# Two mixer layers: exchange of halves issued by SyncE, two pairs of index banks, low-rank products in four row groups, and steps in other places

## What is computed

```
x = x + 0.5 * swiglu(rms_norm(x), ...)
p = rms_norm(x) @ w_in                    # 12 column tiles for attention, 15 for the two recurrences
ya = dsa_attention(pa)                    # index scores pick 128 keys per query, then softmax over them
yb = rwkv7_time_mix(pb); yc = gated_deltanet(pc)
x = x + concat(ya, yb, yc) @ w_out
x = x + 0.5 * swiglu(rms_norm(x), ...)
```

## Time and profile before

| | |
|---|---|
| median of 3 runs | 3539.54 us (3538.71 to 3545.95) |
| profiled execution | 3536.79 us, its span 3535.0 us |
| PE busy | 3386.3 us, 96% of the span |
| mean granted clock of PE | 0.98 |
| first block's projection stretches, layer 0 and layer 1 | 382 to 565.5 us, 1556 to 1740.5 us |

### The profile page before, as it was taken

One profiled execution on the slowest core, in us unless ns is written; L12 is line 12 of the kernel. 1 busy time (PEld: TensorE's weight loads), 2 busy tenths in 40 slices (PEclk: granted clock), 3 DMA queues, 4 the chain that ended last, 5 costly groups with the idle time before them and its releaser, 6 DMA issues.

```text
span 3535.0 us, 47369 instructions
## 1 busy us (share of the span) xinstructions
PE 3386.3 (96%) x16944; PEld 2781.0 (79%) x16944; DVE 1423.5 (40%) x2753; ACT 1255.4 (36%) x1890; POOL 1659.6 (47%) x2052
## 2 busy tenths in 40 slices
PE   7999998799999999999878999999899999999999
PEld 6888776688888888887658788878767888888887
DVE  5431588845221422137886532214563110341100
ACT  4222436434222422234553432223533332433321
POOL 6765542005665566554400366654404555535554
PEclk9999999899999999999989999999999999999999
DMA  5443321003443344333200244432202223213222
GB/s 183 143 147 107 104 87 55 13 7 120 147 145 117 122 146 143 119 104 93 66 25 1 72 148 146 134 108 78 72 1 78 95 95 99 73 66 101 95 98 99
DMA packets 104223, 340.49 MB, mean 96 GB/s; under 512 B 12144, under 2 KB 17936, under 8 KB 103968
## 3 DMA queue, kind: packets, MB, share of 16 engines
q1 hardware_dynamic: 83984, 277.83, 24.0%
q10 hardware_dynamic: 20112, 60.89, 5.4%
HBM read 330.78 MB, written 2.65 MB: 94 GB/s over the span
## 4 chain that ended last, share of the span: by engine, by line
issue 39%; POOL 32%; PE 27%; DVE 1%; POOLq 0%; ACT 0%; DMA 0%; SPq 0%; DVEq 0%
POOL w_lo L667 32%; PE ps L2212 7%; PE ps L2214 7%; PE ps L2213 7%; PE ps L2976 1%; PE ps L2955 1%; PE ps L2235 0%; PE ps L2964 0%; PE ps L2236 0%; PE ps L2240 0%; PE ps L3066 0%; DVE stat L2113 0%; DVE sq L2106 0%; PE ps L3072 0%; PE ps L2956 0%
## 5 line engine op out<-in xcount | busy, mean ns | idle before, releaser
L667 POOL TENSOR_TENSOR w_lo<-w_raw,w_hi 128x256 fp32r<-128x256 f32 x2040 | 1653.0, 842 | 1858.2 <-ACT w_hi L710 1852.5
L2212 PE MATMUL ps<-h_hi,w_hi 128*128 128x512 f32 x2608 | 1021.8, 392 | 1.4 <-ACT mem L938 1.4
L2214 PE MATMUL ps<-h_hi,w_lo 128*128 128x512 f32 x2608 | 1016.9, 390 | 0.0
L2213 PE MATMUL ps<-h_lo,w_hi 128*128 128x512 f32 x2608 | 1016.3, 390 | 0.0
L710 ACT ACTIVATE w_hi<-w_raw 128x1024 fp32r<-128x1024 f32 x510 | 538.3, 1057 | 903.1 <-DMA w_raw<-in_tiles 902.7
L2212 PEld LDWEIGHTS ps<-h_hi,w_hi 128*128 128x128 f32 x2608 | 490.7, 188 | 116.3 <-issue 6.8
L2214 PEld LDWEIGHTS ps<-h_hi,w_lo 128*128 128x128 f32 x2608 | 490.3, 188 | 103.4
L2213 PEld LDWEIGHTS ps<-h_lo,w_hi 128*128 128x128 f32 x2608 | 490.8, 188 | 100.9
L2213 PE MATMUL ps<-a_lo,w_hi 128*128 (+1 forms) x1120 | 437.0, 390 | 0.0
L2212 PE MATMUL ps<-a_hi,w_hi 128*128 (+1 forms) x1056 | 410.8, 389 | 0.0
L2214 PE MATMUL ps<-a_hi,w_lo 128*128 (+1 forms) x1056 | 410.8, 389 | 0.0
(11 more groups left out here) (470 smaller groups left out, 3617.1 us busy)
## 6 DMA issues: line engine op xcount, KB each, us to landing
w_raw<-in_tiles SPq DMA_DIRECT2D x510, 512.0 KB, 3.4
ada_raw<-in_ada_tiles ACTq DMA_DIRECT2D x96, 512.0 KB, 3.4
mem<-mem ACTq DMA_DIRECT2D x80, 64.0 KB, 2.0
x<-in_x_t SPq DMA_DIRECT2D x2, 1024.0 KB, 6.6
sq<-in_cond ACTq DMA_DIRECT2D x4, 512.0 KB, 4.0
mem<-gates SPq DMA_DIRECT2D x8, 256.0 KB, 4.1
consts<-in_consts SPq DMA_DIRECT2D x1, 1280.0 KB, 13.0
core_mem<-gates SPq DMA_DIRECT2D x8, 128.0 KB, 2.8
```

What stands on the lines that cost most here:

```text
L667: ins = nc.gpsimd.tensor_tensor(w_lo[:, s, part], w_raw[:, s, part], w_hi[:, s, part].bitcast(F32), ALU.subtract)
L2212: nc.tensor.matmul(bank, wh, hi, start=first, stop=False, skip_group_check=True)
L2213: nc.tensor.matmul(bank, wh, lo, start=False, stop=False, skip_group_check=True)
L2214: return nc.tensor.matmul(bank, wl, hi, start=False, stop=last, skip_group_check=True)
```

## The change

1. **Exchange of halves.** `swap_halves` moves from ACT's program into SP's. SP issues the four DMAs of a unit behind the load of a tile, once the unit's copy is done; all weight loads behind it in SP's queue follow.
2. **Index pairs.** Odd pairs use banks 2 and 3 and the ReLU buffers `U_Z`; even pairs keep 5, 6 and 43, 44. Waits on ReLUs and sums reach back four instead of two. Pairs 0 and 1 stand behind tile 6, pairs 2 and 3 behind tile 7, pair p behind tile p + 4 from there: the last is behind recurrent tile 3 and not 5.
3. **Low-rank.** The 64 rows of the third product are split into two groups of 32: eight matmuls in four row groups, with one wait between the first four and the last four, since the halves of one sum go to the same bank.
4. **Other places.** Key sums stand inside tile 13 and not behind it; their roots stand before the copy of tile 13, with the Sqrt table loaded earlier; the decays and their wait stand before the last copy; the rounding of the last tile's successor and the copy of `v_first` move into the attention loop. On DVE the rotations of keys and queries go from pairs 1 to 5 to pairs 3 to 7, `head_inverse` from pair 9 to pair 10, and eight selection rounds go ahead of the head scaling.

```diff
+        INDEX_TILES = {6: (0, 1), 7: (2, 3), **{p + 4: (p,) for p in range(4, len(INDEX_PAIRS))}}
+        def index_bank(p):
+            return 2 if p % 2 else 5
+        def relu_unit(p):
+            return U_Z if p % 2 else 43
...
+            def swap_halves(l, m):                                   # SP
+                unit = att_unit(m)
+                r = TURNS.index(unit)
+                if r >= 4:
+                    sp.wait_ge(S["roped"], 10 * l + r - 3)
+                sp.wait_ge(S["proj_out"], (ATT_TILES + REC_TILES) * l + m + 1)
+                turned = mem[:, U_TURNED[unit], :]
+                for at in range(0, P, HD):
+                    for to, of in ((at, at + HD // 2), (at + HD // 2, at)):
+                        sp.dma_start(turned[to:to + HD // 2, :], mem[of:of + HD // 2, unit, :]).then_inc(S[f"rot_moved{r % 4}"], 16)
...
+                load_tiles(start, att + RING)
+                for m in range(ATT_TILES):
+                    load_tile(att + m + RING)
+                    if m == 1:
+                        swap_halves(l, 0)
+                    if m and att_unit(m) in U_TURNED:
+                        swap_halves(l, m)
...
-                        if i >= 2:                                   # ACT, index_relus
-                            act.wait_ge(S["score_added"], i - 1)
-                        nc.scalar.activation(mem[:, 43 + x, 0:w], ps[:, 5 + x, 0:w], ACT.Relu)
+                        if i >= 4:
+                            act.wait_ge(S["score_added"], i - 3)
+                        nc.scalar.activation(mem[:, relu_unit(p) + x, 0:w], ps[:, index_bank(p) + x, 0:w], ACT.Relu)
-                    if att_unit(m) in U_TURNED:
-                        act.wait_ge(S["proj_out"], done)
-                        swap_halves(att_unit(m))
...
+                    if m == LORA_TILE + 1:                           # ACT, before the copy of tile m
+                        head_roots(7, 2, 1.0, EPS_L2)
+                    if m == LORA_TILE + 1:                           # ACT, behind the copy
+                        act.wait_ge(S["decay_in"], l + 1)
+                    if m < REC_TILES - 1:
+                        round_tile(base + m + 4)
+                    if i == 1:                                       # ACT, attention loop
+                        round_tile(BASE[f"rec_in{l}"] + REC_TILES - 1 + 4)
...
-                    if 1 <= p <= 5:                                  # DVE
+                    if 3 <= p <= 7:
-                        rope(U_K + p - 1).then_inc(S["roped"], 1)
+                        rope(U_K + p - 3).then_inc(S["roped"], 1)
-                    if p == 9:
+                    if p == 10:
                         head_inverse(mem[:, 33:38, :], 5)
+                best_keys(2, range(12, 16))
+                best_keys(1, range(4))
                 scale_heads((0, 1))
...
-                        for bank, rows in ((2, slice(0, 32)), (4, slice(32, 64)), (6, slice(64, 128))):
-                            ins = nc.tensor.matmul(ps[:, bank + c, :], lora[rows, l, blk(c)], lg[rows, :], start=True, stop=True)
+                        for row, bank, part in ((0, 2 + c, c), (32, 4 + c, c), (64, 6 + c, c), (96, 7 - c, 1 - c)):
+                            rows = slice(row, row + 32)
+                            ins = nc.tensor.matmul(ps[:, bank, :], lora[rows, l, blk(part)], lg[rows, :],
+                                                   start=row < 64 or c == 0, stop=row < 64 or c == 1, skip_group_check=True)
+                            if c == 0 and row >= 64:
+                                ins.then_inc(S["lora_ready"], 1)
+                                if row == 96:
+                                    pe.wait_ge(S["lora_ready"], 3 * l + 2)
```

More of the change, by code:

```diff
@@ L914, in index_relus @@
                         act.wait_ge(S["index_ready"], i + 1)
[L915 to L928 removed]
+                        if i >= 4:
+                            act.wait_ge(S["score_added"], i - 3)
+                        nc.scalar.activation(mem[:, relu_unit(p) + x, 0:w], ps[:, index_bank(p) + x, 0:w], ACT.Relu).then_inc(S["relu_ready"], 1)
                 for m in range(ATT_TILES):
@@ L2397, in index_scores @@
                         pe.wait_ge(S["roped"], roped0 + 2 + p)
-                    done = due("index", 2) - 2
-                    if done:
+                    done = due("index", 2) - 4
+                    if done > 0:
                         pe.wait_ge(S["relu_ready"], done)
@@ L2417, in attention @@
                         head_sum(m - 8)
-                    if index_pair(m) is not None:
-                        index_scores(index_pair(m))
+                    for p in index_pairs(m):
+                        index_scores(p)
                 due("proj_out", ATT_TILES)
@@ L2444, in attention @@
                         due("roped", 5)
-                    if index_pair(ATT_TILES + m) is not None:
-                        index_scores(index_pair(ATT_TILES + m))
+                    for p in index_pairs(ATT_TILES + m):
+                        index_scores(p)
                     if m == 0:
```

70 lines of the change are left out of this document (27 added, 43 removed).

## The result

| | before | after |
|---|---|---|
| median, runs beside each other | 3541.54 us (3538.71 to 3545.95, 4 runs) | 3514.73 us (3507.53 to 3516.75, 4 runs) |
| ratio, 95% interval | | 0.9923 (0.9908 to 0.9938) |
| profiled execution | 3536.79 us, span 3535.0 | 3516.75 us, span 3514.9 |
| mean granted clock of PE | 0.980 | 0.981 |

One of the ten executions of the run before_again, further down, had a granted clock of 0.55 and took 5705 us; it is left out there.

The account below looks back on a forecast made before the run. PE was taken as the bound, busy 3386 of 3535 us; gains of 8.6 (layer 0) and 9.2 us (layer 1), together 17.8, took 3536.8 to 3519.0, or 3521.7 for the median; own range 3515 to 3528, with rivals 3512 to 3532.

Parts of the forecast that it names:

- copies behind the exchange: Index part: PE's waits for ACT's copies behind the first exchange shrink, gaining 0.4 and 0.3 us in layers 0 and 1.
- ReLU waits at the index pairs: Index scores: PE's waits for ACT's ReLUs go whole with two pairs of banks, 2.6 and 3.2 us.
- half clock behind them and fewer places: Index part: half-clock stretches go with the ReLU waits, 1.7 us a layer; moving pairs itself put at nothing.
- wait at the spread: Spread of head norms: PE's wait for the last ReLU goes, 1.1 us a layer.
- low-rank products: Low-rank group: two slots of four products instead of four slots, 1.8 us gained a layer.
- start of the softmax: Softmax start: last copy comes sooner, most waits turn into one for the next exponentials; 1.0 and 1.1 us gained.
- first rival: Softmax start gives all it has: 6.4 us more from waits, some 3 from the clock, 3512 us; chance 0.12.
- The last sign: Softmax start: PE would then wait 2 us or more for an exponential.
- Exchange on SP: SP issues the halves instead of ACT: 2.4 us an exchange, landing up to 5.4 us, cost nothing.
- Moving pairs changes no count: Index pairs: still 24 small matmuls a layer, so moving them gains or costs nothing in itself.
- VectorE at the spreads: Spreads: DVE's inversion ends at 503.2, PE comes at 506.6, margin 3.4 us; rival that DVE becomes the bound, chance 0.12.
- Selection rounds: Head scaling: eight rounds ahead of it, 9 us, go into time that DVE has.

Follow-up runs that it names:

- before_again: The kernel before with no edit, run once more for a second profile: 3539.5 us, ratio 0.9997 to before.
- a_one: Changed kernel with index pairs one per tile from tile 6, rotations and inversion at their old pairs, second banks kept: 3527.45 us, ratio 0.9959 to before.
- b_sp: Kernel before with only the exchange of halves moved from ACT to SP: 3530.17 us, ratio 0.9963 to before.
- a_act: Changed kernel with the exchange of halves back in ACT's queue, all else kept: 3518.25 us, ratio 0.9933 to before.
- a_new2: Changed kernel with last tile's rounding later, Tanh and Sigmoid earlier, and index pairs in six places instead of ten: 3499.65 us, ratio 0.9886 to before.
- b_lora: Kernel before with only the low-rank products changed, to two slots of four 32-row groups: 3534.62 us, ratio 0.9981 to before.
- a_new: Changed kernel with last tile's rounding moved behind the sixth exponential, Tanh and Sigmoid ahead of a rounding: 3507.81 us, ratio 0.9901 to before.
- a_keys: Changed kernel with DVE's selection rounds back in one block behind the low-rank inputs: 3518.65 us, ratio 0.9940 to before.

## Why the prediction was right, and where it was not

Measured against the profiled executions, in us, layer 0 / layer 1:

| step | forecast | measured | from |
|---|---|---|---|
| copies behind the exchange | 0.4 / 0.3 | 0.5 / 0.0 | waits 0.91 / 0.46 before, 0.46 / 0.46 now; before_again has 0.46 in layer 0 too |
| ReLU waits at the index pairs | 2.6 / 3.2 | 2.6 / 3.2 | waits gone |
| half clock behind them and fewer places | 1.7 and 0 / 1.7 and 0 | 2.9 / 3.1 | rest of the distance to the first spread, 6.6 / 7.5; a_one puts 1.1 of it with the places, which leaves 1.8 / 2.0 |
| wait at the spread | 1.1 / 1.1 | 1.1 / 1.1 | wait gone |
| low-rank products | 1.8 / 1.8 | 1.9 / 1.9 | 20.6 to 18.7; 0.3 more of the wait ahead in layer 1 |
| start of the softmax | 1.0 / 1.1 | 1.3 / -0.5 | last distance; the waits named there fell by 1.4 / 1.4 |

The two stretches and the copies come to 19.5 of the span's 20.1 us, against a forecast of 17.8. The median of 3514.73 us lies in the range of 3512 to 3532, but 0.3 us outside the forecast's own 3515 to 3528, and nearer to the first rival's 3512 than to the forecast's 3521.7. By the total alone that rival would have won; its mechanism is not what the trace shows, since PE still waits 2.7 and 3.0 us at the softmax's start. The signs named were there: no wait at the index scores and the spread, no half clock ahead of the softmax, 2.40 us for the low-rank group, the second scores 1.30 us behind the first. The last sign, 2 us or more for an exponential, came as 1.9 and 2.2 for the copy behind it.

- **Exchange on SP** was right in every row: 2.41 us of issue, landing at 2.1 in the median and 3.4 at most (2.0 and 4.1 before) where I had allowed 5.4, no wait for a rotation and none for a weight's low part. I sized this part as the copies alone, though, and gave the ReLU waits to the second pair of banks. That step failed: b_sp removes the waits of 2.6 and 2.2 us with one pair of banks, a_act leaves 2.2 and 1.4 with two. The rows had said so: 429.69 plus 2.45 is the issue's end, and without it the ReLUs stand at 429.7, before PE comes at 430.8 (its second pair began at 433.42, after 2.59 us of idle time). The wait's end was forecast rightly, and its cause given to the wrong half of the change; that the sum came out is luck in this term, as both halves were in the change. The rule of the Trainium skill that was weighed there ("DMA: Bandwidth & Descriptors", section "Issuing engines are not separate DMA queues", issue time usually small beside the DMA) misleads here: one issue is 0.6 us beside 2.1 to its landing, but the ReLUs stood behind four in a row, 2.45 us, and the exchange moved by itself has a ratio of 0.9963 (0.9949 to 0.9977). By the other rule weighed, that of the Trainium skill's same page on queue rows served in turns, I had argued that the halves would be late behind weight tiles in SP's queue; the 2.1 us show nothing of it.
- **"Moving pairs changes no count"** was true and not enough. This is a term that the sum put at nothing. Each place at which PE leaves the wide products costs 0.4 to 0.5 us beside the products themselves (a_new2, a_one). Two places fewer a layer were worth 2.2 us in all by a_one and up to 2.6 by the rest of the distance, about the 2.3 us by which forecast and profile differ.
- **VectorE at the spreads**: the inversion ended at 503.9 (forecast 503.2), but PE came at 505.2, not 506.6, since it had gained more; 1.4 us of margin, not 3.4. The rival was nearer than its text, and a_one shows its price: 2.0 us of wait and 1.6 of half clock behind it in layer 1.
- **Low-rank products** were sized rightly in themselves. The wait between their two slots, which I had put at 0.2 to 0.3 us, was 0.2: the second slot begins 1.26 us behind the first, where the old slots followed each other by 1.06. The sum took them as independent of the softmax's start, and b_lora shows they are not: alone they are worth nothing in the profile. They also had an effect that the profile of before could not show, since neither of its layers had it: half clock from the midst of the three-group products on, 3.2 us in four of eight layers.
- **Start of the softmax**: the step named what is late next, and it was (L2566, 1.9 and 2.2 us, behind a rounding that waits for a landing). In layer 1 the gain was lost since the products with `v_down` fell into half clock; before, then after:

```profile
1755.66 1.91 PE L2475 MATMUL ps<-mem,v_down 128*32 128x512 f32 x4 [1.79 <-DVE core_mem L1651]
```

```profile
1734.72 3.56 PE L2502 MATMUL ps<-mem,v_down 128*32 128x512 f32 x4 [1.79 <-DVE core_mem L1670]
```

Against before_again, where this distance is 60.1 us and not 57.3, the changed kernel's 57.8 is a gain: the size of this term in layer 1 is not settled. The first rival, that the softmax start gives all it has, was not this change but the next one: a_new.
- **Selection rounds** at no gain and no cost: a_keys.

The 26 us of the medians against 20 of the profiles: the second profile of before is 3.8 us longer, with 3.2 us of half clock at layer 0's low-rank products, which the first profile doesn't have. By the mean spans of the two profiles of each kernel (3536.9 and 3514.2) the gain is 22.7 us. b_lora fits in part: no difference in the first profile, 5 us in the medians. What the other 3 to 4 us are is open; the code behind layer 1's softmax, the same in all fourteen profiles, differs by up to 5 us alone. I don't claim more for it.

## What to carry to other kernels

When two edits each remove the same wait, or when one frees time that the next wait takes, their worth isn't a sum: make one alone and undo one in the whole, and read the distance between two fixed places of the bound engine's timeline, rather than the total. From tile 4 to the low-rank products that distance was 131.2 to 131.8 us in every profile of the changed kernel that left this part alone; where half clock falls otherwise it differs by 2 to 3 us as well (139.6 and 137.1 in layer 1 of the kernel before), so take two profiles. Ask of every in-order engine what it does while it stands before a transfer: four DMA issues ahead of a small step that the bound engine needs cost it 1.4 to 2.6 us of waiting here, and a weight's rounding ahead of one 1.9 to 2.2. And small groups of products are cheaper together than apart, by 0.4 to 0.5 us a place.

## What I had not expected of the hardware

- With all its operands ready PE still fell to half clock in the midst of the low-rank products (four slots with one or two row groups each, 0.51 for 6.8 us, 3.2 us lost) in four of eight layers; with four row groups in each of two slots in none of twenty.
- Not every idle time is followed by half clock: of the index waits, 2.6 us had it each time (three profiles), 2.2 and 2.1 in layer 1 had it, 2.2 and 1.4 in a_act and 1.8 in before_again had not. So the 1.7 us that I counted with each may or may not come.
- The four groups ran side by side: sixteen records of 32 rows in 2.40 us, a wait for the first slot's results among them, where twelve records had taken 4.29.
- Four DMAs from SBUF to SBUF took 2.41 us to issue on SP and 2.44 on ACT, longer than the 2.0 to 2.1 us from one's issue to its landing, on either queue.
